# Order of the column tiles in an input projection: both pooling tiles behind the first recurrent tile

## The reference, cut to what matters

```python
z = h @ w_in                       # columns: z_x 512 | z_g 512 | z_p 256 | z_f 256
u = conv_centred(z_x)              # four taps along the tokens, per channel
r, ig = sigmoid(u @ wa + ba), sigmoid(u @ wx + bx)       # "gates", for both directions
a = exp(-8 * r * softplus(-lam)); b = sqrt(-expm1(2 * log_a)) * (ig * u)
hf, hb = scans of (a, b) forwards and backwards, started from the context's scan states
y_a = (hf + hb) * gelu(z_g)
y_p = (box means over windows 2, 4, 8, 16 on a 16 x 64 grid - z_p) @ pool_w * pool_scale
y_f = 2-D Fourier mixing of z_f
x = x + mod[2] * (concat(y_a, y_p, y_f) @ w_out)
x = x + mod[5] * mixture_of_experts(modulate(rms_norm(x), mod[3], mod[4]))   # 16 experts, 2 per token
```

## Time and profile before

| | us |
|---|---|
| three runs, median (lowest, highest) | 1084.62 (1083.42, 1086.98) |
| the profiled execution, its own time | 1086.46 |
| its span in the trace | 1084.7 |
| PE busy | 900.0 (83%) |
| DVE busy | 718.8 (66%) |
| ACT busy | 415.1 (38%) |
| POOL busy | 392.1 (36%) |

### The profile page before, as it was taken

How to read it: one execution, slowest core, us unless ns; L and a number is a source line. 1 busy time by engine, 2 the same in 40 slices (tenths; PEclk the granted TensorE clock), 3 DMA queues, 4 the chain that set the end, 5 groups by cost and what they waited for, 6 DMA issues and landing times.

```text
span 1084.7 us, 12383 instructions
## 1 busy us (share of the span) xinstructions
PE 900.0 (83%) x3689; PEld 632.3 (58%) x3690; DVE 718.8 (66%) x794; ACT 415.1 (38%) x520; POOL 392.1 (36%) x181
## 2 busy tenths in 40 slices
PE   6789999949798899992379998999999899988800
PEld 2354444414345478882358886888888677767700
DVE  2234778996883353446885778568646988888648
ACT  1333535325436221113242454435414556556212
POOL 1000735910000000003253647156341777766672
PEclk9989999969899999995589998999999888888955
DMA  8884405015205422316555748476452888887494
GB/s 318 292 330 135 176 20 193 0 39 187 105 0 203 184 78 112 117 78 255 188 190 212 279 168 317 159 271 238 158 223 86 317 317 309 325 311 268 168 358 190
DMA packets 96277, 213.48 MB, mean 197 GB/s; under 512 B 11007, under 2 KB 31613, under 8 KB 96253
## 3 DMA queue, kind: packets, MB, share of 16 engines
q1 hardware_dynamic: 85708, 174.37, 43.9%
q0 software_dynamic: 5904, 21.50, 5.5%
q10 hardware_dynamic: 4640, 17.30, 3.9%
HBM read 180.12 MB, written 33.03 MB: 197 GB/s over the span
## 4 chain that ended last, share of the span: by engine, by line
PE 51%; DVE 28%; issue 8%; DVEq 4%; DMA 3%; ACT 3%; POOL 2%; SPq 0%; ACTq 0%; POOLq 0%
PE bank L701 10%; DVE WP L1524 7%; PE bank L908 3%; PE bank L888 3%; PE bank L887 3%; PE bank L886 3%; PE bank L909 3%; PE bank L910 3%; PE bank L814 3%; PE bank L815 3%; PE bank L816 3%; DVE rkt L1538 2%; PE bank L745 2%; PE bank L683 2%; DVE U L1279 2%
## 5 line engine op out<-in xcount | busy, mean ns | idle before, releaser
L621 POOL TENSOR_TENSOR WP<-raw,WP 128x1024 fp32r<-128x1024 f32 x64 | 186.8, 2947 | 0.7 <-ACT WP L1138 0.5
L701 PE MATMUL bank<-hT,wring 128*128 128x512 f32 x384 | 169.3, 600 | 2.6 <-ACT hT L966 1.9
L1524 DVE TENSOR_TENSOR WP<-raw,WP 128x2048 fp32r<-128x2048 f32 x62 | 156.8, 2568 | 11.7 <-ACT WP L1134 8.3
L1134 ACT ACTIVATE WP<-raw 128x2048 fp32r<-128x2048 f32 x64 | 119.5, 1917 | 90.8 <-issue 84.9
L886 PE MATMUL bank<-WP,xp 128*128 128x512 f32 x368 | 144.1, 391 | 1.5 <-DVE xp L1561 1.5
L888 PE MATMUL bank<-WP,xp 128*128 128x512 f32 x368 | 143.8, 391 | 0.0
L887 PE MATMUL bank<-WP,xp 128*128 128x512 f32 x368 | 143.7, 391 | 0.0
L701 PEld LDWEIGHTS bank<-hT,wring 128*128 128x128 f32 x384 | 73.7, 193 | 93.5 <-issue 90.0
L617 POOL TENSOR_TENSOR held<-held 128x1 f32<-128x1 f32 x24 | 36.2, 1508 | 218.7 <-DVE idg L1553 210.8
L633 POOL TENSOR_TENSOR WP<-raw,WP 128x2048 fp32r<-128x2048 f32 x2 | 9.0, 4532 | 283.6 <-ACT WP L1134 283.6
L908 PE MATMUL bank<-WP,hp 128*128 128x512 f32 x184 | 83.2, 452 | 0.0
(11 more groups left out here) (278 smaller groups left out, 1503.6 us busy)
## 6 DMA issues: line engine op xcount, KB each, us to landing
raw<-in_expert_w_gate SPq DMA_DIRECT2D x64, 512.0 KB, 3.9
raw<-in_expert_w_up SPq DMA_DIRECT2D x64, 512.0 KB, 6.4
raw<-in_expert_w_down SPq DMA_DIRECT2D x64, 512.0 KB, 8.1
mring<-in_mod_w SPq DMA_DIRECT2D x20, 1024.0 KB, 5.3
expert_rows<-ysc ACTq DMA_DIRECT2D x23, 512.0 KB, 7.0
expert_rows<-g SPq DMA_DIRECT2D x16, 512.0 KB, 11.4
wring<-in_w_in SPq DMA_DIRECT2D x12, 512.0 KB, 6.0
mslot<-in_mod_w SPq DMA_DIRECT2D x4, 1024.0 KB, 14.9
```

Of the source, the lines that this page charges most:

```text
L621: pool.tensor_tensor(WP[:, j, 1, 2 * D:], raw[:, j, 2 * D:], WP[:, j, 0, 2 * D:].bitcast(F32), ALU.subtract).then_inc(s_lod[j], 1)
L701: mm = pe.matmul(o_, wring[:, n % 3, k, :], src, start=k == 0, stop=k == KD - 1)
L1134: A_(WP[:, j, 0, 0:2 * D], raw[:, j, 0:2 * D], ACT.Copy).then_inc(s_hgu, 1)
L1524: tt(WP[:, j, 1, 0:2 * D], raw[:, j, 0:2 * D], WP[:, j, 0, 0:2 * D].bitcast(F32), ALU.subtract).then_inc(s_logu[j], 1)
```

## The change

The list of column tiles and the two lists that follow it on ACT and DVE are put in another order. No instruction is added or removed, and `MOD_AFTER`, which goes by a tile's index in `COLT`, stays as it is.

```diff
-        COLT = [("x", 0), ("g", 0), ("p", 0), ("x", 1), ("g", 1), ("p", 1), ("x", 2), ("g", 2), ("x", 3), ("g", 3),
+        COLT = [("x", 0), ("p", 0), ("p", 1), ("g", 0), ("x", 1), ("g", 1), ("x", 2), ("g", 2), ("x", 3), ("g", 3),
                 ("f", 0), ("f", 1)]
-        GATES_AFTER = {("p", 0): 0, ("p", 1): 1, ("g", 2): 2, ("g", 3): 3}
+        GATES_AFTER = {("p", 1): 0, ("g", 1): 1, ("g", 2): 2, ("g", 3): 3}
...
             take_x(0)
+            take_p(0)
+            take_p(1)
+            rec_gates(0)
             take_g(0)
             gelu_tanh(0)
-            take_p(0)
-            rec_gates(0)
             take_x(1)
             rec_root(0)
             take_g(1)
             gelu_tanh(1)
-            take_p(1)
             rec_gates(1)
...
             conv(0)
+            mod_sums(2)
+            rec_input(0)
             gelu_poly(0)
-            mod_sums(2)
             gelu_end(0)
-            rec_input(0)
```

## The result

The changed kernel is slower. Its four runs have a median of 1098.85 us (1094.38 to 1101.4) beside 1085.8 us for four runs of the kernel before; the ratio is 1.0112, with a 95% interval of 1.0083 to 1.0141. A second build of it, six more runs, gave 1.0076 (1.0047 to 1.0105). The forecast was +11 us, a ratio of 1.010: 1095.6 us, with a range of 1087.5 to 1101.

A forecast was written before the change was run, and what follows sets the result against it. From about 173 to 223 us DVE, delayed by POOL's box means, was taken to bound the stage. PE's wait, conv(1)'s POOL waits, restart and gelu moved mod_end(5, 0) by +11.2, round +11: 1084.62 + 11 = 1095.6 us, range 1087.5 to 1101.

The forecast's parts named there:

- mark A: Start of `mod_end(5, 0)` on DVE, forecast at 234.4 us instead of 223.19, +11.2.
- The order up to gates(0), and mod_sums(2): PE's tiles up to gates(0), and DVE's mod_sums(2) ahead of gelu_poly(0): both forecast to cost nothing.
- POOL moves forward: Box means on POOL start at 101.1 us, run back to back and lie on conv(1), whose waits cost 11.5 us.
- the signs of the prediction: Expected profile after the change, including POOL busy without a gap from about 101 to nearly 179 us.
- The wait on PE: PE stands 19 us between x1 and the product (2, 1), waiting for mod_end(2, 0) behind conv(1).
- the kernel without this wait: Rival case: no PE wait at the product, POOL's waits still on conv(1); +5.6 us, 1090; no chance given.
- a turn in scan(0): DVE's rec_scan(0) was given 1.5 us for its first turn with POOL.
- POOL's new place: Box means beside conv(1) on DVE, said to carry about half of the forecast.
- Faster: both costs stay away: Rival: product (2, 1) doesn't hold PE and conv(1) runs alone; -7.4 us, 1077.2; chance 0.05.
- The restart at the lower clock: PE's product and g1 after the idle run some 5 us at half speed, costing 2.5 us.
- gates(1) waits for gelu: Gates(1) follow g1's take, polynomial 1.95 us and tanh 1.06, which p1 covered before; gates end at 210.5 us.

The follow-up runs named there:

- late_product: Changed kernel with the product (2, 1) after the tile with index 5 (g1) instead of 4 (x1); ratio 1.0052 to the kernel before.
- late_product_no_box_means: Changed kernel with the product (2, 1) after index 5 and POOL's box means left out; median 1100.7 us, with other routing.
- late_gates_first: Changed kernel with the product (2, 1) after index 5 and gates ahead of tanh for tiles 1, 2 and 3; ratio 0.9927 to the kernel before.
- changed_box_means_held: Changed kernel with POOL's second box means held until conv(1) is done; ratio 1.0083 to the kernel before.
- before_gates_first: Kernel before, with rec_gates(2) and (3) ahead of gelu_tanh on ScalarE and rec_input(i + 1) ahead of gelu_end(i + 1) on VectorE; ratio 0.9953.
- before_no_box_means: Kernel before, with POOL's box means left out; median 1088.4 us, with other routing.

## Why the prediction was right

The steps of the prediction, counted from the start of the second z tile:

| step | forecast | measured |
|---|---|---|
| x1's end on PE | 72.1 | 71.4 |
| conv(1) starts, lasts | 73.4, 16.9 | 72.8, 16.1 |
| PE's idle ahead of the product | 19 | 18.2 |
| g1's end (with the slower clock after the idle) | 108.4 | 107.1 |
| gates(1) end | 124.1 | 122.4 |
| conv(2) starts | 142.6 | 141.1 |
| mark A | 148.0 | 146.4 |
| difference to before | +11.2 | +9.6 |

*The order up to gates(0), and mod_sums(2).* Held. gates(0) ended 39.5 us after the start of the second z tile, 0.4 sooner than before. The chunks of mod_sums(2) came later than DVE wanted them, but the sum was over at 115.8, before the gates' first half at 121.5.

*POOL moves forward.* Held in kind: back to back, and each of conv(1)'s six instructions waited, 10.8 us in all for a forecast of 11.5. Even the polynomial's first half took a turn (4.50 us for 0.69). POOL's own work was priced too high, though. It ended at 172.71, 87.8 us after the start of the second z tile, where the signs of the prediction had nearly 179, which is 92.6. Even so its last instruction was still there to hold up the last one of conv(1), which ended 1.1 us later, at 173.79. That the waits came out nearly as large as forecast is in part luck.

*The wait on PE.* Held in place and size, and late_product shows that it matters. The prediction, though, says what each part is worth, and there it was off. It put the kernel without this wait at +5.6, so the wait at half the loss. late_product measured +2.5 at A: the wait is worth 7.0 of 9.6. The terms at fault are conv(1), 0.8 shorter and 0.6 sooner, which lowered both kernels alike, and 1.5 us for a turn in scan(0) which wasn't there, since POOL had ended at 172.7, before the scan began at 174.3. In the forecast of the changed kernel that turn sat beside g1, where scan(0) had slack, and so it did not show.

The prediction also laid the other half on "POOL's new place". As a difference to the kernel before, that doesn't hold: the new place is the cheaper one by 3.2 us (10.6 against 13.8 in the old), and what costs beside the product is the order itself, 5.5 us. The sums behind that sentence had this right. The rival "Faster: both costs stay away" gave -7.4 us at A for a kernel without the wait and with conv(1) alone, and late_product_no_box_means, which is such a kernel (with POOL quiet everywhere), measured 128.54 - 136.76 = -8.2.

*The restart at the lower clock.* Forecast 2.5 us. Measured 1.02 on the product and 1.68 on g1, 2.7. The granted clock after the change, in stretches of 2 us (PE busy, clock, DMA share, GB/s; 1.00 is 2.4 GHz and 0.50 is 1.2):

```profile
158.00:160.00 2.00, 0.00 (x0) 0.82 0.00 0
...
172.00:174.00 2.00, 0.00 (x0) 0.50 0.00 0
176.00:178.00 2.00, 2.00 (x3) 0.50 0.00 0
178.00:180.00 2.00, 2.00 (x4) 0.56 0.00 0
180.00:182.00 2.00, 2.00 (x6) 1.00 0.00 0
```

PE stopped at 156.32. The clock fell to 1.2 GHz between 158 and 160, was there when the product began at 174.54, and was back at 2.4 GHz between 178 and 180, some 5 us later, as in the earlier trace rows.

*gates(1) waits for gelu.* Held: 2.68 us of idle ahead of ACT, and the tanh at 195.09. This is the larger part of the 5.5 us that the order costs with POOL and product set aside: three of them went away in late_gates_first, when the gates no longer stood behind the tanh (139.3 to 136.2). The rest was not taken apart. In late_gates_first, with POOL's turns on conv(1), gates(1) still stands for 6.21 us, now behind the end of scan(0); in the order of before p1 lay between g1 and gates(1) and covered this too.

*Whole time.* The stage gives +10 us at B. The two comparisons gave 1.0112 (+12.2 us) and 1.0076 (+8.3), so the forecast of +11 lies between two builds of the same kernel, and how close it comes to either is chance in part. Take the difference in time to the kernel before, and from it the difference at B. What is left is +2.1 and -1.8 us for these two, +2.6 for late_product, -1.4 for changed_box_means_held, +0.6 for before_gates_first and -0.9 for late_gates_first: it lies on both sides. It is largest between two kernels without box means: late_product_no_box_means took 12.3 us longer than before_no_box_means, while the stage shows 5.8 at B. What follows the stage isn't changed by any of these edits, and its span varied between 783.3 and 787.0 us in the seven profiled executions of kernels with the box means. Whether part of what is left is real, by other phases of the DMAs, or chance of one profile each, is not settled.

## What to carry to other kernels

When a list of work is reordered, look for what goes by position and doesn't move along: here a table by index left a product behind a tile whose result it needed, and PE stood for 18 us in the middle of its busiest stretch. Before pricing such a stall in full, ask what would be waited for next, since 11 of those 18 us would have been lost ahead of the moved product and inside the gates anyway. Long work on GpSimd that takes turns with VectorE wasn't free at any of the places tried here, in all of which VectorE was on the chain. Whether it would be free where VectorE idles was not tried. Look also for a wait on the chain for work that the next consumer doesn't need: gates ahead of gelu gained 5.7 us at B in the old order, while the new order, with the product and gelu put right, gained only 1.3 us of the stage beyond that.

## What the runs showed of the hardware

Beside POOL a `tensor_scalar` with one SBUF input took 4.50 us for 0.69 (the changed kernel, at 139.43), and in changed_box_means_held scans took 4.48 for 0.69 (256 columns) and 5.47 for 2.35 (1024 columns). So the turns also take in an instruction with a single input, and scans, beside the additions and multiplications with two inputs that the trace of before showed. `mod_end`, which reads one input from PSUM and one from SBUF, kept its 0.67 us at 198.76 in changed_box_means_held, while POOL was in its additions. (The Trainium skill, "SBUF — State Buffer", "Who interferes with whom", says that `tensor_scalar` can enter the modes in which VectorE takes the port pair that it shares with GpSimd, and that an instruction with at most one SBUF input outside these modes doesn't contend; the 4.50 us and the 0.67 us agree with it.)
